# Hybrid SSD/S5 decoder step, one Trainium2 core: the in-chunk taps of the S5 scan contracted as four lags by 32 features

## The reference, cut to what matters

```python
lam_bar = jnp.exp(lam * step)
b_bar = ((lam_bar - 1.0) / lam)[..., None] * lax.complex(b_re, b_im)
ug = u.reshape(bt, L, S5_GROUPS, S5_GROUP)          # 64 groups of 16 features
bu = jnp.einsum('gnk,blgk->blgn', b_bar, ug)        # 64 complex states a group
# states[l] = lam_bar * states[l-1] + bu[l]
y = jnp.real(jnp.einsum('gkn,blgn->blgk', c, states)) + d.reshape(S5_GROUPS, S5_GROUP) * ug
```

## Time and profile before

| | |
|---|---|
| median of 3 runs | 1071.95 us (1071.65 to 1072.99) |
| the profiled execution | 1076.74 us, of which the span in the trace is 1075.0 us |
| PE busy | 939.4 us (87% of the span) |
| DVE, ACT, POOL busy | 473.7, 335.4, 55.6 us |
| mean granted TensorE clock | 0.928 of full |
| DMA packets | 82069, 297.70 MB; under 512 B 20030 |
| the chain that ended last, by engine | PE 65%, DMA 25%, DVE 5% |
| the same by line, the largest of the S5 part | none of its lines is among the first sixteen; the experts' weights are 12%, 7% and 5% |

### The profile page before, as it was taken

One profiled execution on the slowest core, in us unless ns is written; L12 is line 12 of the kernel. 1 busy time (PEld: TensorE's weight loads), 2 busy tenths in 40 slices (PEclk: granted clock), 3 DMA queues, 4 the chain that ended last, 5 costly groups with the idle time before them and its releaser, 6 DMA issues.

```text
span 1075.0 us, 16048 instructions
## 1 busy us (share of the span) xinstructions
PE 939.4 (87%) x6687; PEld 632.0 (59%) x6687; DVE 473.7 (44%) x797; ACT 335.4 (31%) x672; POOL 55.6 (5%) x82
## 2 busy tenths in 40 slices
PE   8989999999999999999999999767678587677474
PEld 6778478995579999988878744323223223132121
DVE  5999945667677445556565410200102020202023
ACT  5333155566476245553444421100000000000002
POOL 2701300010100000000000000000000000000000
PEclk9989999999999999999999989968878788879798
DMA  9581450345462744524799779999999999999994
GB/s 272 138 211 47 154 197 2 119 139 172 138 211 100 303 157 151 205 80 157 262 358 355 307 311 401 430 428 427 428 427 427 429 428 429 426 427 422 427 422 154
DMA packets 82069, 297.70 MB, mean 277 GB/s; under 512 B 20030, under 2 KB 29978, under 8 KB 67533
## 3 DMA queue, kind: packets, MB, share of 16 engines
q1 hardware_dynamic: 79508, 289.30, 69.7%
q0 software_dynamic: 2112, 7.28, 2.0%
q10 hardware_dynamic: 376, 0.10, 0.0%
HBM read 286.76 MB, written 9.90 MB: 276 GB/s over the span
## 4 chain that ended last, share of the span: by engine, by line
PE 65%; DMA 25%; DVE 5%; SPq 2%; issue 1%; ACT 1%; DVEq 0%; ACTq 0%
DMA ring<-in_w_exp_down_dram 12%; PE bank L2257 7%; DMA ring<-in_w_exp_gate_dram 7%; DMA ring<-in_w_exp_up_dram 5%; PE bank L1909 5%; PE bank L1910 5%; PE bank L1911 5%; PE bank L1500 5%; PE bank L1515 5%; PE bank L2275 4%; PE bank L2303 3%; PE bank L1524 3%; PE bank L1800 2%; PE bank L1699 2%; PE bank L1920 2%; PE bank L1921 1%
## 5 line engine op out<-in xcount | busy, mean ns | idle before, releaser
L2257 PE MATMUL bank<-ring,work 128*32 128x512 f32 x704 | 141.8, 710 | 67.6 <-DMA work<-in_w_exp_up_dram 21.6
L2257 PEld LDWEIGHTS bank<-ring,work 128*32 128x32 f32 x704 | 34.9, 127 | 154.3 <-issue 122.9
L1909 PE MATMUL bank<-ops,usplit 128*128 128x320 f32 x368 | 114.5, 311 | 1.1 <-DVE usplit L2778 1.1
L1910 PE MATMUL bank<-ops,usplit 128*128 128x320 f32 x368 | 113.9, 310 | 0.0
L1911 PE MATMUL bank<-ops,usplit 128*128 128x320 f32 x368 | 113.9, 309 | 0.0
L2275 PE MATMUL bank<-ring,work 128*32 128x512 f32 x416 | 67.3, 714 | 40.2 <-DMA ring<-in_w_exp_down_dram 27.7
L2778 DVE TENSOR_TENSOR usplit<-ring,usplit 128x2048 fp32r<-128x2048 f32 x31 | 71.0, 2290 | 52.9 <-ACT usplit L1186 52.9
L3105 DVE TENSOR_TENSOR work<-bank,g 128x512 f32<-128x512 f32 x7 | 4.8, 692 | 202.0 <-PE bank L2303 202.0
L2257 PE MATMUL bank<-work 128*32 128x512 f32 x304 | 87.9, 712 | 0.0
L1515 PE MATMUL bank<-work,ring 128*128 128x320 f32 (+1 forms) x304 | 78.7, 417 | 1.1 <-issue 1.1
L1186 ACT ACTIVATE usplit<-ring 128x2048 fp32r<-128x2048 f32 x32 | 61.5, 1922 | 41.7 <-PE bank L1911 31.6
(11 more groups left out here) (513 smaller groups left out, 1648.2 us busy)
## 6 DMA issues: line engine op xcount, KB each, us to landing
ring<-in_w_exp_down_dram SPq DMA_DIRECT2D x20, 2048.0 KB, 19.9
ring<-in_w_exp_gate_dram SPq DMA_DIRECT2D x18, 2048.0 KB, 16.4
ring<-in_w_exp_up_dram SPq DMA_DIRECT2D x16, 2048.0 KB, 20.0
ring<-in_w_in_dram SPq DMA_DIRECT2D x10, 2048.0 KB, 9.9
work<-in_w_exp_up_dram SPq DMA_DIRECT2D x8, 2048.0 KB, 28.8
work<-in_w_exp_gate_dram SPq DMA_DIRECT2D x6, 2048.0 KB, 21.8
ring<-in_w_exp_gate_dram SPq DMA_DIRECT2D x11, 1024.0 KB, 7.8
ring<-in_w_glu_dram SPq DMA_DIRECT2D x4, 2048.0 KB, 8.7
```

The costliest lines, as they stand in the source:

```text
L1909: nc.tensor.matmul(b[:, 0:T], wh, hi_[:, k], start=(k == 0), stop=False)
L1910: nc.tensor.matmul(b[:, 0:T], wh, lo_[:, k], start=False, stop=False)
L2257: ins = nc.tensor.matmul(psum[part][ES * x:ES * (x + 1), :], xs[i % 2][:, kk, x], wt[x][:, k], start=(kk == 0), stop=(kk == KT - 1))
```

## The change

The eight lags become two groups of four. For a tile ft and a strip k of 32 output features, one matmul contracts 128 rows = 4 lags x 32 input features at once, so a tile takes eight matmuls of 32 stationary columns: four strips with 320 moving columns (lags 0 to 3) and four with 160 (lags 4 to 7). For that the moving operand `ux` has to hold four copies of the input, each 40 columns further to the right, with zeros (POOL's memsets) in front. SP reads these copies from the scratch in DRAM: 16 DMAs for a tile (4 lags x 4 strips), each into 32 partitions, in pieces of 160 bytes. `ux` has four buffers of one tile each, so tiles 4 to 7 wait for fy0 to fy3. The taps go through `tapm` (DVE) and 16 DMAs that bring the four lags of a group one under the other into `ks`. All 144 new DMAs stand in SP's queue between blocks: tiles 0 to 2 between mv1 and xbc0, `ks` and tiles 3 to 7 between xbc1 and xbc2. The taps jobs move up behind xbc0, all of chunk_out moves ahead of chunk_sum, `yT` gets four buffers, and xhi, xlo and the first weight splits change place on DVE and ACT. Several semaphores are merged; DVE's wait for the b matrices becomes a wait for all nine S5 loads.

```diff
-    j += ["xbc0", "xbc1", "dtT", "xbc2", "dt3", "xbc3"]
-    j += ["ye0", "yo0", "kk0", "ye1", "yo1"]
+    j += ["xbc0", "kk0", "kk1", "xbc1", "dtT", "xbc2", "dt3", "xbc3"]
+    for n in range(4):
+        j += [f"ye{n}", f"yo{n}"]
     for ft in range(KT):
         j += [f"fy{ft}", f"ty{ft}"]
...
-        kbd = [view(ring[:, 17408:21504], (4, Q, P)), w(13056, 4, Q, P)]
+        tapm, ks = w(13056, Q, KT, 2 * S5K), w(15104, 4, 2, KT, 2 * S5K)
+        ux = [view(ring[:, 17408 + 4 * T * i:17408 + 4 * T * (i + 1)], (4, T)) for i in range(3)] + [w(13056, 4, T)]
...
-            for n in range(BIDX["mk1"], BIDX["z1"] + 1):
-                load_block(n)
+            def lagged_in(ft):
+
+                rows_of = scr.rearrange("(s f) (j t c) -> s f j t c", s=4, j=Q, t=KT)
+                for lag in range(4):
+                    for k in range(4):
+                        sp.dma_start(ux[ft % 4][32 * lag:32 * lag + 32, k, NCK * lag:T].rearrange("p (j c) -> p j c", c=NCK),
+                                     rows_of[k, :, 0:Q - lag, ft]).then_inc(s[f"ux{ft % 4}"], 16)
+
+            load_block(BIDX["mk1"])
+            load_block(BIDX["mv0"])
+            load_block(BIDX["mv1"])
+            sp.wait_ge(s["uxz"], 1)
+            for ft in range(3):
+                lagged_in(ft)
+            load_block(BIDX["xbc0"])
+            load_block(BIDX["xbc1"])
+            sp.wait_ge(s["tapm"], 1)
+            for k in range(4):
+                for lag in range(4):
+                    sp.dma_start(ks[32 * lag:32 * lag + 32, k], tapm[32 * k:32 * k + 32, 3 - lag::4]).then_inc(s["s5_in"], 16)
+            sp.wait_ge(s["uxz"], 2)
+            lagged_in(3)
+            for ft in range(4, KT):
+                got(sp, f"fy{ft - 4}")
+                lagged_in(ft)
+            load_block(BIDX["xbc2"])
+            load_block(BIDX["z0"])
+            load_block(BIDX["z1"])
...
# POOL, behind hi7 and ahead of sls
+            lagged = ring[:, 17408:17408 + 12 * T].rearrange("p (a n) -> p a n", n=T)
+            for lag in range(1, 4):
+                ins = pool.memset(lagged[32 * lag:32 * lag + 32, :, 0:NCK * lag], 0.0)
...
+            pool.wait_ge(s["s5_in"], 16 * (Q + 16))
+            pool.wait_ge(s["sls"], 1)
+            for lag in range(1, 4):
+                ins = pool.memset(ux[3][32 * lag:32 * lag + 32, :, 0:NCK * lag], 0.0)
...
# ACT
+            conv_silu(2)
             chunk_states(0)
-            conv_silu(2)
+            chunk_states(1)
             conv_silu(3)
-            chunk_states(1)
+            chunk_states(2)
+            chunk_states(3)
...
-                if ft in (2, 4):
-                    chunk_states(ft // 2 + 1)
-                if ft == 4:
+                if ft == 1:
                     pair_high(0)
-                if ft == 5:
+                if ft == KT - 1:
                     pair_high(1)
...
# PE, chunk_sum
-                pe.wait_ge(s["kbd"], ft + 1)
-                for d in range(Q):
-                    ins = nc.tensor.matmul(b[:, NCK * d:T], kbd[ft // 4][:, ft % 4, Q - 1 - d], u5T[:, 0:Q - d, ft],
-                                     start=(d == 0), stop=(d == Q - 1))
+                pe.wait_ge(s["s5_in"], 16 * (Q + 16))
+                pe.wait_ge(s[f"ux{ft % 4}"], 256 * (ft // 4 + 1))
+                for late in range(2):
+                    cols = T // 2 * late
+                    for k in range(4):
+                        ins = nc.tensor.matmul(b[32 * k:32 * k + 32, cols:T], ks[:, k, 1 - late, ft], ux[ft % 4][:, k, 0:T - cols],
+                                               start=(late == 0), stop=(late == 1))
...
-            chunk_out(0)
-            taps(0)
-            chunk_out(1)
+            for n_ in range(4):
+                chunk_out(n_)
             for ft in range(KT):
                 chunk_sum(ft)
...
# DVE
-            dve.wait_ge(s["ld_b"], 32)
+            dve.wait_ge(s["ld_s5"], 16 * 9)
...
+            def lag_taps(i):
+
+                job, sts = f"kk{i}", slice(4 * i, 4 * i + 4)
+                got(dve, job)
+                tap = bank(job)[:, :].rearrange("p (f q k) -> p q f k", f=4, q=Q)
+                for h_ in range(2):
+                    ins = TS(tapm[:, :, sts, S5K * h_:S5K * (h_ + 1)], tap, par2[:, h_:h_ + 1], None, ALU.mult)
+                emptied(ins, job)
+                done(dve, job)
+                for ft in range(4 * i, 4 * i + 4):
+                    ins = STT(out=tapm[:, Q - 1, ft], in0=fold4[:, :], scalar=vec[:, V_D5 + ft:V_D5 + ft + 1], in1=tapm[:, Q - 1, ft],
+                              op0=ALU.mult, op1=ALU.add)
...
-            for ft in range(6):
-                block_taps(ft)
+            got(dve, "yo1")
+            q(dve.tensor_copy(xhi, hnT))
+            got(dve, "yo3")
+            TT(xlo, hnT, xhi.bitcast(F32), ALU.subtract).then_inc(s["xlo"], 1)
```

More of the change, by code:

```diff
@@ L263 @@
 SEMS = (
[L265 to L271, removed]
+    "ld_vec ld_par ld_x ld_xs ld_u50 ld_mem ld_small ld_s5 ld_st0 ld_st1 ld_st2 ld_st3 ld_k0 ld_k1 ld_k2 ld_v0 ld_v1 ld_v2 ld_gain "
+    "dve act pool consts ss var rs0 rooted xn s5w s5c btab rtab rot hprev sls ctab tapm uxz ux0 ux1 ux2 ux3 xc convout "
+    "u5_out s5_in "
+    "ehi elo tap0 xlo zs dtx sp_e dt_ready cs_in wdec bblk zf ze csm mt y_done ysq yr yn glu_used "
     "whi wlo hn_hi hn_lo yb_hi yb_lo u5_hi u5_lo mrg_hi mrg_lo q_hi q_lo ao_hi ao_lo diag rsb ssq rsn tn wrg nmax prn nmax_s pexp_s sb_full ob_full osb zeroed lgT rt_lg nm rt_a rt_e rt_m rt_d rt_x window npass "
     "raw_rest raw_last half_unit unit_done half_done hg rsf fnq fys sil hid sel selw side4 side5 side6 side7 got4 got5 got6 got7 y_a y_b pass_done fy "
-        "out_kv out_s5 out_st0 out_st1 out_st2 out_st3 out_hl ss_fin out_y0"
+        "out_s5 out_st0 out_st1 out_st2 out_st3 out_hl ss_fin out_y0"
 ).split()
@@ L1565, in _ @@
                     tr(par[:, 0:124], vecrow[0:124], 124)
-                    pe.wait_ge(s["rows"], 1)
+                    pe.wait_ge(s["s5w"], 1)
                     for i in range(3):
@@ L1647, in _, with taps @@
             al = [ones[:, :], ones[:, :], same_s[:, :, :].rearrange("p b l -> p (b l)")]
+            def taps(i):
+                b = take(f"kk{i}")
+                for st in range(HST * i, HST * (i + 1)):
+                    k, f = st % 4, st // 4 % 4
+                    for ri in range(2):
+                        ins = nc.tensor.matmul(b[32 * k:32 * k + 32, P * f:P * (f + 1)],
+                                               bx[:, ri, st].rearrange("p h k -> p (h k)"),
+                                               ctab[i][:, st % HST, ri, 1:Q + 1].rearrange("p q k -> p (q k)"),
+                                               start=(ri == 0), stop=(ri == 1))
+                end(ins, f"kk{i}")
             pe.wait_ge(s["rot"], 1)
@@ L1650, in _ @@
                 proj("xbc", m, hnT, T)
+                if m == 0:
+                    for i in range(2):
+                        pe.wait_ge(s["ctab"], i + 1)
+                        taps(i)
                 if m == 1:
@@ L1680, in chunk_out @@
                                     end(ins, f"y{'eo'[h_]}{n_}")
[L1682 to L1692, removed]
             def chunk_sum(ft):
                 b = take(f"fy{ft}")
[L1697 to L1702 removed]
+                pe.wait_ge(s["s5_in"], 16 * (Q + 16))
[5 more added lines that the diff above has]
+                                               start=(late == 0), stop=(late == 1))
+                end(ins, f"fy{ft}")
                 b = take(f"ty{ft}")
@@ L2635, in _ @@
                     TT(dte, dtx, dtm, ALU.min).then_inc(s["dtx"], 1)
-            def block_taps(ft):
-                job = f"kk{ft // 4}"
-                if ft % 4 == 0:
-                    got(dve, job)
-                out = kbd[ft // 4][:, ft % 4].rearrange("p q (g k) -> p q g k", g=8)
-                tap = bank(job)[:, P * (ft % 4):P * (ft % 4 + 1)].rearrange("p (q k) -> p q k", q=Q)
-                mask = sel16[:, :, :].rearrange("p a b -> p (a b)")
-                ins = TT(out, tap.unsqueeze(2).to_broadcast([P, Q, 8, S5K]),
-                         mask.unsqueeze(1).unsqueeze(3).to_broadcast([P, Q, 8, S5K]), ALU.mult)
-                if ft % 4 == 3:
-                    emptied(ins, job)
-                    done(dve, job)
-                else:
-                    q(ins)
-                own = kbd[ft // 4][:, ft % 4, Q - 1]
-                STT(out=own, in0=ident[:, :], scalar=vec[:, V_D5 + ft:V_D5 + ft + 1], in1=own, op0=ALU.mult, op1=ALU.add)\
-                    .then_inc(s["kbd"], 1)
             def chunk_outputs(ft):
```

90 lines of the change are left out of this document (43 added, 47 removed).

## The result

The changed kernel takes 1110.76 us (median of 4 runs, 1109.49 to 1112.09), the kernel before 1072.47 us beside it (1071.65 to 1076.28): ratio 1.0345, 95% interval 1.0325 to 1.0365. That is 38.3 us slower. The sign of the forecast was right, and its 1085 us and its range to 1100 were too low.

The account below looks back on a forecast made before the run. The prediction took PE as the bound from 133 to 195 us, with SP's issues to limit tiles 4 to 7 after the change. 8.9 (ty7 later) + 3.0 (clock) + 1.0 (DVE's wait) = +12.9 us, so 1085 us, range 1073 to 1100.

Parts of the forecast that it names:

- The sign of the forecast: Whole kernel: slower, +12.9 us; chance of slower 0.84, faster 0.13, same 0.03.
- PE's gain: Chunk sums on PE: 22.6 us removed, 7.2 added, so PE alone would gain 15.4 us.
- the cost of a piece: Lagged copies on the DMA engines: 19 ns of an engine for each piece, 0.25 us a DMA.
- VectorE's wait: DVE's start on the b matrices: also waiting for the c matrices costs +1.0 us (0 to 3.5), carried to the end.
- transfers set the pace: Rival for the copies: issuing takes 0.25 us, SP isn't the limit, kernel faster at 1066 us; chance 0.13.
- pieces set the pace: Rival for the copies: from 35 ns a piece the DMA engines are slower than SP; 1107 to some 1285 us; chance 0.08.
- The price of issuing: SP's queue: each added DMA takes 0.456 us to issue (0.37 to 0.55), so a tile costs 7.3 us of SP.
- the ug row: Eight small DMAs from the same scratch, nothing queued ahead, 3.65 us to issue; the source of 0.456 us each.
- a block lands 7.7 us after its issue: Weight block xbc0: issued at 128.1, landed at 135.8, so PE, wanting it at 133.32, waits 2.5 us.
- the formula of the rivals: End of ty7: 165.2 + max(0, 48c - 19.4) + 64c + 3.7, with c as SP's time a DMA.
- Just in time: Before the first chunk sum: SP finishes ks and lagged_in(3) by 166.4, ahead of fy0's end at 167.6.
- The clock behind it: PE after the waits of tiles 4 to 7: a lower granted clock following idle time costs +3.0 us (0 to 4).

Follow-up runs that it names:

- xbc0 ahead of tiles 1 and 2: Changed kernel with only SP's issue order altered: tile 0's copies, block xbc0, tile 1's copies, block xbc1, tile 2's copies; 1099.48 us, ratio 1.0244.
- long pieces: Changed kernel with the same 128 copies read from a second scratch ordered by tile, in runs of 800 to 1280 bytes; 1096.31 us, ratio 1.0226.
- extra matmuls in the waits: Changed kernel plus 16 matmuls of 128x128 into an unused PSUM bank ahead of each sum of tiles 4 to 7; 1110.79 us, ratio 1.0359.
- tiles 4 to 7 not copied: Changed kernel without the 64 copies of tiles 4 to 7, sums reusing tiles 0 to 3; 1574.19 us, not comparable (other experts chosen); +10.3 at the mark.

## Why the prediction was right or wrong

**Right: the mechanism and the sign.** SP's queue became the limit of tiles 4 to 7, PE stood for the copies, xbc0 came late, and PE's gain was eaten. The chunk sum (1.02 us against 0.9), the cost of a piece (15 ns against 19), landing behind an issue (1.8 to 2.9 us against 2.7) and the first step of VectorE's wait (mv1 1.0 us later) came out about as worked. Some of the last is luck: mv1's issue differs by 1.0 us between profiles of the same program up to there. The rivals "transfers set the pace" and "pieces set the pace" were both wrong about what they name: the DMA engines are busy 0.37 to 0.44 there.

**Wrong: the size of SP's terms**, by which ty7 was forecast at 200.5 and came at 223.24. The chain of the forecast, term by term:

| term of the forecast | forecast, us | measured, us | difference |
|---|---|---|---|
| issue of mv1 (VectorE's wait, priced apart) | at 105.9 | at 106.9 | +1.0 |
| 48 issues | 21.9 | 29.0 | +7.1 |
| xbc0 from issue to PE's start | 7.7 | 10.3 | +2.6 |
| from there to tapm | 12.2 | 13.9 | +1.7 |
| 16 issues for ks | 7.3 | 10.8 | +3.5 |
| their landing, memsets | 3.7 | 2.7 | -1.0 |
| lagged_in(3) | 7.4 | 10.1 | +2.7 |
| idle until fy0 | 1.2 | 0 | -1.2 |
| 64 issues | 29.2 | 34.8 | +5.6 |
| last issue to ty7's end | 3.7 | 4.4 | +0.7 |

The differences add up to 22.7 us. 18.9 of them are one step, "The price of issuing": c = 0.456 from the ug row for every DMA that is added. In the trace there are three prices. Copies of lags 1 to 3 take 0.44 to 0.45 us in the median, near my value. Those of lag 0 with 256 pieces take 0.607 and ks's, from SBUF to SBUF, 0.60 (0.67 from one to the next). And the first sixteen, right behind mv1's 2 MB, took 11.6 us, 0.72 each, with landings up to 7.9 us. xbc0 ahead of tiles 1 and 2 shows the same three times (11.6, 10.6 and 15.6 us). It goes with two things together, a block that drains ahead and many short pieces: the sixteen copies with long pieces stand behind the same block and take 7.5. A row of eight with nothing ahead of it could show none of this. The long pieces measure both parts together (14.5 us at the median); what holds the queue up behind a block stays open.

The second step is smaller: "a block lands 7.7 us after its issue" is the row of a block alone in the queue. Late as it is, xbc0 goes out beside xbc1 and the store of mv, and takes 10.3.

A larger c alone would not have done. The mean of the first 48 is 0.60; in the formula of the rivals even that value for all gives 165.2 + 28.8 - 19.4 + 38.4 + 3.7 = 216.7, 6.5 us short, because the formula takes ks and tile 3 as covered by PE and starts the late copies at fy0. At their real prices they weren't covered: "Just in time" is the sentence that failed there. SP ran from 160.5 to 218.9 with a single gap and never waited for fy0.

**The clock behind it** was forecast at +3.0 and the offset grew by 3.9 from ty7 to the mark: 35.5 - 31.6. The size holds, the reason only in part, so some of it is luck. The extra matmuls in the waits brought 2.3 us of it back. But with tiles 4 to 7 not copied the clock fell as well, without long waits, and in the changed kernel it fell when the first of them had only just begun.

**VectorE's wider wait.** DVE in order of time:

```profile
34.74 0.91 DVE L2559 TENSOR_TENSOR work<-work,s5p 128x512 f32<-128x512 f32 x1 [2.69 <-DMA ring<-in_s_c_im_dram]
```

It starts at 34.74 (35 forecast, 31.77 in the earlier trace rows). That was +1.0 at mv1, as forecast, and nothing that could be measured at the end of this kernel. I carried it through one to one, past a wait with a clock transition behind it, and that was wrong.

**A sum of a rival.** At 157 ns a piece the prediction's own formula, with c = 2.04, ends ty7 at 165.2 + 78.5 + 130.6 + 3.7 = 378.0 and the kernel at some 1262 us; "about 400" and "some 1285" don't follow from it. Nothing here depends on them.

## What to carry to other kernels

When work moves from an engine to many small DMAs, count DMAs first, bytes second: here SP's queue mostly paid 0.42 to 0.67 us for each, and 0.43 for one that carried four times 33 KB, and the same change with 32 copies in place of 128 turned +38 us into -3.9. Price a queue by a row of the same kind (size and number of pieces), with the same thing ahead of it; the shortest row of a quiet queue is a lower end, not the middle. And write down the queue's whole program around the change: what stands behind the added issues (here a weight block, and 16 more small copies) pays for all of them.

## What the runs showed of the hardware that I had not expected

- A DMA's issue cost depends on its access pattern: 607 ns with 256 pieces of 160 bytes, 437 to 447 with 224 or fewer (but 600 for the one right behind a copy of 256 pieces), 421 with one long run a row, and 430 for a three-dimensional one of four times the bytes, all medians.
- Behind a 2 MB block that is still being moved, sixteen copies with short pieces took 10.6 to 15.6 us to issue against 8.5 without a block ahead; sixteen with long pieces took 7.5 behind the same kind of block and 7.4 without one.
- Two queues issue such copies side by side at nearly the price of one alone (0.55 and 0.56 us against 0.54; over all 32 of each queue 0.58 and 0.59), with the DMA engines' share at 0.74 in place of 0.37 to 0.44.
- The granted clock can fall to 0.50, the level of 1.2 GHz, while PE is busy 9.45 of 10 us, in the stretch of matmuls with 32 stationary columns and transposes of 40 rows. Three matmuls of 128x128 ahead of each sum held it at 1.00 in 166 to 186 us. The median fell by 4.3 us (1069.38 to 1065.05); in the profiles the way from mv1's issue to the mark is 2.1 us shorter.
